# Modulation sums: transposes for one-column products, two sums of a part on TensorE, and other orders in the first pairs

## The reference, cut to what matters

```python
def adaln(cond, w, b):                     # w is (1024, 9 * 1024) for each layer
    m = jax.nn.silu(cond) @ w + b
    return m.reshape(cond.shape[0], 1, N_MOD, D_MODEL)

def modulate(x, g, shift, scale):
    return rmsnorm(x, g) * (1.0 + scale) + shift

def ffn_half(x, m, j, g, wg, wu, wd):
    h = modulate(x, g, m[:, :, j], m[:, :, j + 1])
    return x + 0.5 * m[:, :, j + 2] * ((jax.nn.silu(h @ wg) * (h @ wu)) @ wd)

for l in range(2):
    x = ffn_half(x, m, 0, ...)                                     # ffn0, ffn2
    x = x + m[:, :, 5] * mixer(modulate(x, norm_g[l, 1], m3, m4))  # even, odd
    x = ffn_half(x, m, 6, ...)                                     # ffn1, ffn3
y = rmsnorm(x, final_g)
```

## Time and profile before

| | before |
|---|---|
| median of 3 runs | 2732.85 us (2731.78 to 2735.22) |
| the profiled execution | 2735.34 us |
| its span | 2734.0 us |
| mean granted clock of TensorE | 0.978 of 2.4 GHz |
| PE busy | 2601.6 us (95%), 17539 instructions |
| DVE busy | 1707.8 us (62%) |
| ACT busy | 1065.7 us (39%) |
| POOL busy | 1028.7 us (38%) |
| moved from and to memory | 253.66 and 3.82 MB |

### The profile page before, as it was taken

One profiled execution on the slowest core, in us unless ns is written; L12 is line 12 of the kernel. 1 busy time (PEld: TensorE's weight loads), 2 busy tenths in 40 slices (PEclk: granted clock), 3 DMA queues, 4 the chain that ended last, 5 costly groups with the idle time before them and its releaser, 6 DMA issues. The chain is left out here.

```text
span 2734.0 us, 43460 instructions
## 1 busy us (share of the span) xinstructions
PE 2601.6 (95%) x17539; PEld 2506.0 (92%) x17539; DVE 1707.8 (62%) x2789; ACT 1065.7 (39%) x1740; POOL 1028.7 (38%) x725
## 2 busy tenths in 40 slices
PE   6999999899998999989899898999999999999998
PEld 5999999899766898989899898999899989999998
DVE  5565466724677656767686585868565556656473
ACT  4221122234466453333336341424442446343343
POOL 2453344334200353424243542424332224453443
PEclk8999999999999999999999999999999999999999
DMA  7433442431200112434231233333221111122222
GB/s 274 154 122 128 160 144 88 159 99 55 72 1 1 47 62 93 136 96 139 94 123 63 93 112 120 112 105 109 90 75 55 40 62 62 62 85 75 88 74 74
DMA packets 205075, 259.90 MB, mean 95 GB/s; under 512 B 4964, under 2 KB 160232, under 8 KB 204904
## 3 DMA queue, kind: packets, MB, share of 16 engines
q1 hardware_dynamic: 204232, 254.88, 28.2%
q10 hardware_dynamic: 672, 2.62, 0.3%
HBM read 253.66 MB, written 3.82 MB: 94 GB/s over the span
## 5 line engine op out<-in xcount | busy, mean ns | idle before, releaser
L2475 POOL TENSOR_TENSOR wl<-raw,wh 128x512 fp32r<-128x512 f32 (+1 forms) x440 | 621.4, 1442 | 936.5 <-ACT wh L2598 867.9
L2598 ACT CAST wh<-raw 128x2048 fp32r<-128x2048 f32 (+2 forms) x122 | 210.5, 1725 | 567.3 <-PE psU L3342 446.6
L3338 PE MATMUL psU<-hh,wh 128*128 128x386 f32 (+1 forms) x896 | 208.8, 314 | 11.3 <-POOL wl L2475 8.6
L3338 PE MATMUL psG<-hh,wh 128*128 128x386 f32 x880 | 206.6, 316 | 1.1 <-DVE hl L3309 1.1
L3342 PE MATMUL psU<-hh,wl 128*128 128x386 f32 (+1 forms) x896 | 206.9, 312 | 0.0
L3340 PE MATMUL psU<-hl,wh 128*128 128x386 f32 (+1 forms) x896 | 206.7, 312 | 0.0
L3342 PE MATMUL psG<-hh,wl 128*128 128x386 f32 x880 | 202.8, 312 | 0.0
L3340 PE MATMUL psG<-hl,wh 128*128 128x386 f32 x880 | 202.5, 311 | 0.0
L2529 POOL TENSOR_TENSOR wl<-wsum,wh 128x512 fp32r<-128x512 f32 x54 | 70.3, 1302 | 310.1 <-ACT wh L2729 310.1
L2970 DVE SCALAR_TENSOR_TENSOR x<-psU,hgate,x 128x128 f32<-128x128 f32 (+3 forms) x216 | 81.6, 433 | 139.9 <-PE psU L3342 139.9
L3338 PEld LDWEIGHTS psU<-hh,wh 128*128 128x128 f32 x896 | 139.2, 191 | 14.1 <-POOL wl L2475 9.4
(11 more groups left out here) (683 smaller groups left out, 7303.8 us busy)
## 6 DMA issues: line engine op xcount, KB each, us to landing
mraw<-in_mod_w SPq DMA_DIRECT2D x64, 1024.0 KB, 6.6
raw<-in_ffn_w_gate SPq DMA_DIRECT2D x44, 1024.0 KB, 5.2
raw<-in_ffn_w_up SPq DMA_DIRECT2D x44, 1024.0 KB, 5.1
raw<-in_ffn_w_down SPq DMA_DIRECT2D x44, 768.0 KB, 4.4
raw<-in_odd_w_in SPq DMA_DIRECT2D x12, 1024.0 KB, 5.1
raw<-in_even_w_in SPq DMA_DIRECT2D x9, 1024.0 KB, 5.2
raw<-in_ffn_w_down SPq DMA_DIRECT2D x6, 1024.0 KB, 5.0
raw<-in_ffn_w_down SPq DMA_DIRECT2D x8, 640.0 KB, 4.2
```

Source lines behind the costliest of these rows:

```text
L2475: ins = nc.gpsimd.tensor_tensor(wl[:, slot, piece], raw[:, slot, piece], wh[:, slot, piece].bitcast(F32), ALU.subtract)
L2598: nc.scalar.copy(wh[:, slot, 0:width], raw[:, slot, 0:width]).then_inc(w_hi, 1)
L3338: nc.tensor.matmul(ps, lhs_h, rhs_h[:, lo:hi], start=first, stop=False)
```

## The change

1. `mod_turn` makes eight transposes of `macc` (against `ident`) into psA and psB instead of eight one-column products; DVE's `mod_reduce` then sums over their columns in two reductions and adds the bias.
2. `MOD_PLAN` has three places in each part of feed-forwards 1 and 2 instead of two, with one pair each, and the last output part of feed-forward 0 has one pair instead of three. At the first place (behind unit 2) and at the second (ahead of the output tiles) PE makes the sums itself (`mod_rows`): 32 products with `cs` as the stationary side and 128 columns of `mraw` as the moving one, in four column groups of psA. ACT copies the result (`rows_out`), PE turns it with one transpose (`mod_rows_turn`) and DVE adds the bias (`rows_add`). At the third place DVE sums as before, half a pair behind the third output tile and half behind the fifth, and the turn stands behind the seventh.
3. In even units ACT's kept copy stands ahead of the high part of the last product and waits for another sum (`quad_ok`). The low part of the first output weights is made by DVE in one instruction (`down_low`). The output tiles take their six product tiles in the order 1, 0, 3, 2, 5, 4, each with its own wait.
4. In the first pairs ACT's `split` of the second up unit stands ahead of the last two of the eight input pieces, POOL's three `zl` pieces stand behind the first output weights' low part, and two products get their low part on DVE. PE starts four output tiles with their first two products (two of them in banks that were free, `runs_aside`) before it goes on with the others, and the residuals, sums and low parts behind them stand in another order on DVE.

The diff, cut to its core:

```diff
...
-MOD_PLAN = {0: (12, 6, 10, 6), 1: (2, 4, 2, 4, 2, 2), 2: (2, 4, 2, 2, 2, 2), 3: (0, 0, 0, 0, 0, 0)}
+MOD_PLAN = {0: (12, 6, 10, 2), 1: (2,) * 9, 2: (2,) * 8 + (0,), 3: (0,) * 9}
...
+                    place = {1: 0, 2 * PART_PAIRS - 1: 1}.get(j)
+                    if place is not None:
+                        modulation(part, place)
...
+                    if i == 1:
+                        modulation(part, 2)
...
-                for m in range(2):
-                    product_lo(FT * f + 2 * i + m, m, 2 * i + m)
-                if i == 0:
-                    pool.wait_ge(zh_ok, DT * f)
-                    pool.wait_ge(sum_ok, 4 * f)
-                    for kh, h in ((0, 0), (1, 0), (1, 1)):
-                        nc.gpsimd.tensor_tensor(zl[:, kh, h], zf[:, kh, h], zh[:, kh, h].bitcast(F32),
-                                                ALU.subtract).then_inc(zl_ok, 1)
+                    for m in range(2):
+                        product_lo(FT * f + m, m, m)
+            pool.wait_ge(zh_ok, DT * f)
+            pool.wait_ge(sum_ok, 4 * f)
+            for kh, h in ((0, 0), (1, 0), (1, 1)):
...
-                    else:
-                        split_lo(down_unit(f, part, 0), base % 2, PART_TILES * PAIR)
...
+            def rows_out(part, place):
+                mods, q0 = mods_of(f, part, place)
+                if mods:
+                    act.wait_ge(macc_ok, q0 + 2)
+                    nc.scalar.copy(macc[:, 0, 0:P], psA[:, 0:P]).then_inc(mrow_ok[0], 1)
...
-                if j and not up:
-                    product_high(part, j // 2 - 1, 0)
...
+                elif j:
+                    act.wait_ge(quad_ok, 3 * (u - 1) + 2)
                 else:
                     act.wait_ge(seven_prod, 2 * q)
                 act.wait_ge(seven_mm, 7 * u + 1)
                 nc.scalar.copy(dest[:, 0, 0:HT], quad_bank(ps, 0)).then_inc(kept_ok, 1)
+                if j and not up:
+                    product_high(part, j // 2 - 1, 0)
...
+                        if k == 5:
+                            act.wait_ge(up_mm, t + 2)
+                            split(base + 3)
+                else:
+                    act.wait_ge(up_mm, t + 2)
+                    split(base + 5)
...
-            nc.vector.tensor_tensor(mod[:, :, col], psA[:, 0:8].rearrange("p (c t) -> p c t", c=2),
+            for c in range(2):
+                ins = nc.vector.tensor_reduce(mred[:, c], (psA, psB)[c][:].rearrange("p (t b) -> p t b", b=P), AX.X, ALU.add)
+                if c == 0:
+                    st.mark(ins)
+                else:
+                    st.link(ins)
+            nc.vector.tensor_tensor(mod[:, :, col], mred[:],
...
+            def product_low(k):
+                dve.wait_ge(a_hi, FT * f + k + 1)
+                nc.vector.tensor_tensor(act_lo(k), af[:, k % 2, SH:WID], act_hi(k).bitcast(F32), ALU.subtract).then_inc(a_lo, 1)
...
+            def down_low(part):
+                n = down_unit(f, part, 0)
+                whole = slice(0, PART_TILES * PAIR)
+                dve.wait_ge(w_hi, n + 1)
+                dve.wait_ge(w_lo, n)
+                nc.vector.tensor_tensor(wl[:, n % 2, whole], raw[:, n % 2, whole], wh[:, n % 2, whole].bitcast(F32),
+                                        ALU.subtract).then_inc(w_lo, 1)
+
+            def rows_add(q0):
+                dve.wait_ge(mturn_ok, q0 + 2)
+                col = slice(2 * q0, 2 * q0 + 4)
+                nc.vector.tensor_tensor(mod[:, :, col], psB[:, 0:P].rearrange("p (t r) -> p r t", r=32)[:, 0:2, :],
...
-                unit_mods(part, 4 * j)
...
-            for s in range(4):
-                input_sum_lo(s)
-                residual(s // 2, s % 2, rb)
+            for k in range(2, HEAD_TILES):
+                product_low(k)
+            input_sum_lo(0)
+            input_sum_lo(1)
+            residual(0, 0, rb)
+            input_sum_lo(2)
+            residual(0, 1, rb)
+            input_sum_lo(3)
+            residual(1, 0, rb, True)
             first_low(1, 0)
             first_sums(1, 0)
+            residual(1, 1, rb, True)
...
-                    if i < 2 and mods:
-                        mod_sum(q0, 0, i)
...
+                        if mods and m == 0 and 1 <= i <= 2:
+                            mod_sum(q0, 0, i - 1)
+                        if mods and m == 0 and i == 3:
                             mod_reduce(q0)
-                    if i >= 2 and mods > 2:
-                        mod_sum(q0, 1, i - 2)
+                    if i == 0 and mods_of(f, part, 1)[0]:
+                        rows_add(mods_of(f, part, 1)[1])
...
-                    ins = nc.tensor.matmul(psA[:, 4 * c + t:4 * c + t + 1], macc[:, c, t * P:(t + 1) * P], one, start=True, stop=True)
+                    ins = turn((psA, psB)[c][:, t * P:(t + 1) * P], macc[:, c, t * P:(t + 1) * P])
             ins.then_inc(mturn_ok, 2)
+
+        def mod_rows(q0):
+
+            pe.wait_ge(mred_ok, q0)
+            for s in range(2):
+                pe.wait_ge(mod_in[s], (q0 - MOD_HEAD) // 2 * 16 + 16)
+                for k in range(MOD_K):
+                    for g in range(4):
+                        ins = nc.tensor.matmul(psA[32 * g:32 * g + 2, 0:P], cs[:, s * MOD_K + k], mraw[:, s, k, g * P:(g + 1) * P],
+                                               start=s == 0 and k == 0, stop=s == 1 and k == MOD_K - 1)
+                ins.then_inc(macc_ok, 1)
+
+        def mod_rows_turn(n):
+
+            pe.wait_ge(mrow_ok[0], n)
+            turn(psB[:, 0:P], macc[:, 0, 0:P]).then_inc(mturn_ok, 2)
...
+            for m in range(2):
+                pe.wait_ge(res_ok[m], rb)
+                pe.wait_ge((g_scaled, u_scaled)[m], old_tiles(f) + HEAD_TILES)
+                for t in (m, m + 2):
+                    for k in range(2):
+                        if t == 0:
+                            pe.wait_ge(a_lo, tiles_before(f, 0) + k + 1)
+                        head_products(t, k, runs_at[t])
...
+                    if rows and j == 2:
+                        mod_rows(q0)
+                    if rows and j == 3:
+                        mod_rows_turn(turned_rows[f, part])
...
+                        for at, k in enumerate((1, 0, 3, 2, 5, 4)):
+                            if i == 0 and m == 0:
+                                pe.wait_ge(a_lo, tiles_before(f, part) + at + 1)
+                            ins = part_products(w_part(wh, n % 2, k, m), w_part(wl, n % 2, k, m), act_hi(k), act_lo(k),
+                                                runs_alone((psG, psU)[m]), at == 0, at == PART_TILES - 1)
+                        ins.then_inc(down_mm[m], 1)
+                        if i == 0 and m == 1 and rows:
+                            mod_rows_turn(turned_rows[f, part] + 1)
+                        if i == 3 and m == 0 and mods_of(f, part, 2)[0]:
+                            mod_turn(mods_of(f, part, 2)[1])
...
```

More of the change, by code:

```diff
@@ L328, in seven_index, with mods_of @@
         return SEVEN_UNITS * (f - 1) + 2 * PART_PAIRS * (part - 1) + j
+    def mods_of(f, part, place):
+        at = 3 * (part - 1) + place
+        return MOD_PLAN[f][at], MOD_BASE[f, at]
     def down_unit(f, part, i):
@@ L393, in head_rows @@
         ins.then_inc(mrow_ok[side], 1)
+    turned_rows = {}
+    for f in (1, 2, 3):
+        for part in range(1, N_PARTS + 1):
+            turned_rows[f, part] = 2 * len(turned_rows) + 3
     proj_mm = [sem("proj_mm0"), sem("proj_mm1")]
@@ L2414, in seven_ffn_load @@
                     pair_unit(seven_unit(f, part, j), HEAD_PAIRS + PART_PAIRS * (part - 1) + j // 2, j % 2)
-                    if j == 1 and plan[2 * part - 2]:
-                        if part == 1:
-                            sp.wait_ge(sum_lo, 4 * f)
-                        for s in range(2):
-                            modulation(2 * part - 2, 0, s)
+                    place = {1: 0, 2 * PART_PAIRS - 1: 1}.get(j)
+                    if place is not None:
+                        modulation(part, place)
                 k0 = HEAD_TILES + PART_TILES * (part - 1)
@@ L2425, in down @@
                               w_down[:, k0:k0 + PART_TILES, f, i * PAIR:(i + 1) * PAIR])
-                mods = plan[2 * part - 1]
                 for i in range(4):
                     down(i)
-                    if i == 1 and mods:
-                        for s in range(2):
-                            modulation(2 * part - 1, 0, s)
-                    if i >= 2 and mods > 2:
-                        modulation(2 * part - 1, 1, i - 2)
+                    if i == 1:
+                        modulation(part, 2)
         for name in phases:
@@ L3141, in unit @@
                 last_sum(part, j)
+                if j == 4 and mods_of(f, part, 0)[0]:
+                    rows_add(mods_of(f, part, 0)[1])
                 dve.wait_ge(seven_mm, 7 * u + 2)
```

98 lines of the change are left out of this document (51 added, 47 removed).

## The result

The changed kernel takes 2632.43 us (median of four runs, 2628.80 to 2634.94) against 2734.03 us for the kernel before (median of four too): the ratio is 0.9628, with a 95% interval of 0.9611 to 0.9645. The prediction was 2626 us in a range of 2605 to 2654. A second measurement of the changed kernel, on the chip of the last two experiments, gave 2633.3 us (0.9629, 0.9613 to 0.9645).

A forecast was written before the change was run, and what follows sets the result against it. TensorE (PE) was taken as the bound. Terms 23.3 + 30.9 + 18.5 + 4.9 + 25.2 - 3.0 + 7.3 = 107.1 us less gave 2626 us from the 2732.85 median, range 2605 to 2654.

The forecast's parts named there:

- the likeliest case: Whole kernel: every wait goes as counted, time within 12 us of the forecast; chance 0.56.
- The turn: Modulation sums: eight transposes take 0.9 us where eight one-column products took 1.70, gaining 0.83 us in each of 20 turns.
- The row sum: PE's 64 records for a modulation pair: 1.75 us, set by columns, plus 0.1 for one transpose; 12 of them.
- rival A: Row sums: a record has a fixed price, so each costs PE 3.6 us; 22 us more, 2648 us; chance 0.13.
- Feed-forward 0: 15 cheaper turns (12.5 us), two pairs moved away and two half-clock periods gone (2.6): 23.3 us less.
- The 8.2 us of the two pairs: Feed-forward 0's last output part: waits and turns that go when its second and third turns' pairs move away.
- Units and output tiles: Feed-forwards 1 to 3, priced by feed-forward 3 as control: gains of 30.9, 18.5 and 4.9 us.
- The heads: First pairs of feed-forwards 1 to 3: 24.1 us of waits go, 1.5 lost to late DVE, 2.6 half-clock gained: -25.2.
- rival C: First pairs: their waits come back elsewhere through DVE and POOL, half to all of 24.1 us; 2638 to 2650; chance 0.14.
- The last parts: Last output parts: feed-forward 1 +3.0 us, with a 2.0 us turn wait and half-clock periods; feed-forward 2 -7.3, 43.7 against 51.0.
- Rival B: Clock falls behind the new turns or row sums: 2642 behind 12, 2668 behind 32, 2652 by the transpose rule; chance 0.14.
- Rival D: Row sums: PE waits for modulation weight transfers, some 10 us at each of 12; 2746 us, slower than before; chance 0.02.

The follow-up runs named there:

- the last two experiments: Changed kernel with a third row sum in feed-forward 1's last output part, 2629.02 us; with that, GpSimd's second wait and earlier feed-forward 0 loads together, 2618.11 us.
- the two experiments on them: Changed kernel with the first pair of each part summed by VectorE in the units again, 2674.88 us; with only ScalarE's old order in even units, 2633.22 us.

## Why the prediction was right, and where its sizes were off

The forecast was of the likeliest case, every wait as counted, and its sum of 107.1 us met 102.2. By its steps:

1. The turn was forecast at 0.9 us and takes 0.80. Alone it gives 25 us where 32 turns save 29, since the waits for sums and residuals grow.
2. The row sum was forecast at 1.75 us and takes 1.86; the choice of columns over records was right, and rival A (3.6 us, 2648 us) is out.
3. Feed-forward 0: 23.3 forecast, 26.3 measured. 15 turns at 0.90 us less are 13.5. (The 8.2 us of the two pairs are 8.1 by the forecast's own terms.) Most of the extra gain is clock: five pieces of the last output part ran at half clock before, one does now, where I counted two as going. And such a piece costs 1.6 us and not the 1.3 that I took from one short window: the output tile at 487.67 takes 6.04 us to the next one's start, one at full clock 4.40. Against it stands the wait that I had not seen coming, 3.6 us where 2.0 stood: the shorter turns bring PE to a residual earlier than VectorE, whose sum waits for a transfer.
4. Units and output tiles: 54.3 forecast for the three feed-forwards, 52.9 measured. The control inside the run, feed-forward 3, gave this term: what a stretch takes without modulation work, plus what PE adds. Its 74.2 us for the first stretch are 74.35 by its own terms (75.65 - 1.3), and 73.9 measured. That VectorE's sums made the waits in the even units, and not ScalarE's order, is shown by the two experiments on them. Of the change's third item the new order of ScalarE therefore gained nothing. Whether DVE's low half of the first output weights covers the wait in feed-forward 3 was a step of its own; taking it back costs the 3.1 us of the earlier trace rows.
5. The heads: 25.2 forecast, 17.0 measured. This is the term that was mis-sized. The old waits went as counted, with 5.3 us of waits less in each head, but I wrote that the waits of the first pairs end in a lateness of VectorE of 0.5 us each, and it is 2.7, with a piece at half clock behind it (1.6 us) for which I had counted nothing. My adding of durations took VectorE's product at its duration of before (1.93 us), measured where GpSimd stood still, though the same change moves GpSimd's pieces beside it. That was rival C, and a third of its price came: 8.1 of 24.1 us. With GpSimd's pieces held back the time is 2624.48 us.
6. The last parts: in feed-forward 1 the turn waits 1.45 us, where 2.0 were forecast, but no half-clock piece follows there, while the one behind the wait of 2.3 us in the kernel before is gone: -0.2 instead of +3.0. In feed-forward 2, 45.3 us where 43.7 were forecast; the forecast left out a wait of 2.7 us ahead of the mixer's first unit, which stands in both kernels (2.73 and 2.72 us).

Rival B is out: the mean clock rose to 0.991, and no piece at half clock stands behind a turn or a row sum of the changed kernel. Rival D is out: PE waits for no modulation transfer behind the start.

## What to carry to other kernels

When an order is changed so that two engines now work side by side, durations taken from a trace in which one of them stood still are too short: look at who is beside whom in the new order, and price a product from SBUF on VectorE beside GpSimd by a row where both were busy. A stretch of the same run that lacks the work in question is the best measure of what removing it gives. And work that goes from a path with waits can give less than its own length (here 25 of 29 us), since what is late next, a sum, a residual or a transfer, is one or two us behind it.

## What the runs showed of the hardware

Sixty-four records with a two-column stationary side in four column groups take 1.86 us at 128 columns and 3.63 at 256: the time goes with the columns. Eight transposes in a stream of products leave the granted clock at 1.00. Four products of VectorE with both inputs in SBUF take 1.93 us alone and 5.95 beside GpSimd, two differences 1.56 and 3.79; an instruction of 512 columns and one of 128 lose the same 1.0 us. After a wait of 3.64 us a row sum ran at half clock, 3.47 us. Stages that the edits don't touch still differ between runs: in the thirteen traces the even mixer takes 402.8 us (with 10 us of it at half clock) to 406.5 (with 20), the odd one 319.6 or 321.2 (with none, or with one piece of 3.4 us at half clock), and the first two heads of the changed kernel 82.6 to 84.8. A gain below that isn't read from one trace.
